# One plain up panel instead of two in each MLP of a two-block transformer kernel, with products summed in one PSUM bank

## What is computed

```python
def rms_norm(x, g):
    xf = x.astype(jnp.float32)
    y = xf * lax.rsqrt(jnp.mean(xf * xf, axis=-1, keepdims=True) + EPS)
    return (y * g.astype(jnp.float32)).astype(x.dtype)

def sq_relu_mlp(h, w_up, w_down):
    return jnp.square(jax.nn.relu(h @ w_up)) @ w_down

    for layer in range(DEPTH):
        ...
        h = h + sq_relu_mlp(rms_norm(h, g_mlp[layer]), w_mlp_up[layer], w_mlp_down[layer])
```

## Time and profile before

| | |
|---|---|
| median of three runs | 1628.29 us (1628.01 to 1630.63) |
| the profiled execution | 1630.15 us, of which the span from first to last instruction is 1628.4 us |
| TensorE busy | 1598.7 us, 98% of the span |
| VectorE, ScalarE, GpSimd busy | 1016.4, 725.8, 271.0 us |
| mean granted TensorE clock | 0.998 |
| TensorE's lines in the MLP | L1650 (products), L1674 (plain panels), L1703 (down panels) |

### The profile page before, as it was taken

The page is one execution under the profiler, slowest core; times in us unless marked ns, Lnnn a source line. Parts: engine busy times, 40 slices in busy tenths (PEclk is TensorE's granted clock), DMA queues, the critical chain, the costliest instruction groups (busy, mean ns, idle before and its releaser), DMA issues.

```text
span 1628.4 us, 29172 instructions
## 1 busy us (share of the span) xinstructions
PE 1598.7 (98%) x12203; PEld 1417.2 (87%) x12203; DVE 1016.4 (62%) x1416; ACT 725.8 (45%) x1144; POOL 271.0 (17%) x222
## 2 busy tenths in 40 slices
PE   8999999999999999999999999999999999989998
PEld 7998677899999999999887898888887788667896
DVE  6534666388666666555557867677756547856544
ACT  5533554465444444331235544444445445675323
POOL 1002212132222222110004222222212000000200
PEclk9999999999999999999999999999999999999999
DMA  6231030123332222232232333222256676001001
GB/s 197 78 78 31 22 84 10 54 78 130 104 104 89 94 84 99 84 99 93 88 104 78 130 104 104 96 90 100 97 103 99 118 96 89 19 1 62 28 28 52
DMA packets 122689, 134.29 MB, mean 82 GB/s; under 512 B 18877, under 2 KB 99508, under 8 KB 122564
## 3 DMA queue, kind: packets, MB, share of 16 engines
q1 hardware_dynamic: 122362, 132.44, 29.7%
...
## 4 chain that ended last, share of the span: by engine, by line
PE 91%; DVE 4%; ACT 2%; issue 1%; DMA 1%; SPq 1%; ACTq 0%; DVEq 0%
PE ps L483 30%; PE ps L1703 22%; PE ps L1650 17%; PE ps L2699 2%; PE ps L829 2%; PE ps L1674 2%; PE ps L812 2%; PE ps L939 1%; PE ps L1220 1%; PE ps L2427 1%; PE ps L837 1%; PE ps L3224 1%; PE ps L2871 1%; PE ps L2850 1%; PE ps L2866 1%
## 5 line engine op out<-in xcount | busy, mean ns | idle before, releaser
L453 ACT ACTIVATE w_hi<-raw 128x1024 fp32r<-128x1024 f32 (+2 forms) x171 | 179.4, 1051 | 400.4 <-PE ps L483 249.4
L483 PE MATMUL ps<-x_hi,w_hi 128*128 128x512 f32 (+4 forms) x872 | 245.8, 333 | 0.5 <-DVE x_lo L503 0.4
L483 PE MATMUL ps<-x_lo,w_hi 128*128 128x512 f32 (+4 forms) x872 | 239.7, 326 | 0.0
L483 PE MATMUL ps<-x_hi,w_lo 128*128 128x512 f32 (+4 forms) x872 | 239.1, 325 | 0.0
L460 DVE TENSOR_TENSOR w_lo<-raw,w_hi 128x1024 fp32r<-128x1024 f32 (+2 forms) x171 | 206.5, 1222 | 45.1 <-ACT w_hi L453 45.1
L1703 PE MATMUL ps<-a_hi,w_hi 128*128 128x258 f32 (+1 forms) x768 | 204.2, 320 | 0.3 <-DVE h L1887 0.3
L1703 PE MATMUL ps<-a_hi,w_lo 128*128 128x258 f32 (+1 forms) x768 | 204.1, 320 | 0.0
L1703 PE MATMUL ps<-a_lo,w_hi 128*128 128x258 f32 (+1 forms) x768 | 204.0, 320 | 0.0
L483 PEld LDWEIGHTS ps<-x_hi,w_hi 128*128 128x128 f32 (+2 forms) x872 | 145.4, 187 | 19.2 <-issue 3.1
L483 PEld LDWEIGHTS ps<-x_lo,w_hi 128*128 128x128 f32 (+2 forms) x872 | 144.6, 186 | 16.4 <-issue 2.2
L483 PEld LDWEIGHTS ps<-x_hi,w_lo 128*128 128x128 f32 (+2 forms) x872 | 144.6, 187 | 14.7
...
## 6 DMA issues: line engine op xcount, KB each, us to landing
raw<-in_w_mlp_up SPq DMA_DIRECT2D x32, 1024.0 KB, 5.3
raw<-in_w_mlp_down SPq DMA_DIRECT2D x32, 1024.0 KB, 5.0
raw<-in_w_in SPq DMA_DIRECT2D x16, 1024.0 KB, 9.6
raw<-in_w_in_conv SPq DMA_DIRECT2D x12, 1024.0 KB, 5.0
raw<-in_w_in_attn SPq DMA_DIRECT2D x8, 1024.0 KB, 5.2
raw<-in_w_out_attn SPq DMA_DIRECT2D x4, 1024.0 KB, 5.0
raw<-in_w_out_conv SPq DMA_DIRECT2D x4, 1024.0 KB, 4.9
raw<-in_w_out SPq DMA_DIRECT2D x4, 1024.0 KB, 5.8
```

The lines of the kernel that those rows point to most:

```text
L453: act.activation(split_tile(w_hi, t), raw_tile(t), ACT.Copy).then_inc(w_hi_ok, 1)
L483: ins = pe.matmul(tile_banks(t)[0:m, b, 0:c], w[:, k, :], x[:, k, x0:x0 + c], start=(k == order[0] and n == 0), stop=(k == order[-1] and n ...
```

## The change

`PLAIN` goes from 2 to 1: up panel 1 of each layer is made of products too. All four groups of mixtures are started during the out projection (the hi part and remainder of the last one follow it), and the weight parts of panel 1 are made under panel 0. The order of the products is 1, 7, 6, 2, 5, 4, 3 now, on three banks: 6, 5 and 3 all add onto bank 0, ScalarE copies product 1 from bank 0 into bank 1 (in PSUM) before 6 starts, and 2 adds onto that copy. VectorE is left with two additions, and evicts two quarters straight from PSUM with relu and scale.

```diff
-        s1, s7, s6, s75 = [at(n, t_off + 1056 * i, [P, HW]) for i, n in enumerate(("s1", "s7", "s6", "s75"))]
+        s7, s6 = [at(n, t_off + 1056 * i, [P, HW]) for i, n in enumerate(("s7", "s6"))]
...
-        ORDER = (1, 5, 7, 2, 6, 3, 4)
+        ORDER = (1, 7, 6, 2, 5, 4, 3)
...
-        P_BANK = {1: 0, 6: 0, 2: 1, 7: 2, 4: 2, 5: 3, 3: 3}
+        P_BANK = {1: 0, 6: 0, 5: 0, 3: 0, 2: 1, 7: 2, 4: 2}
...
-        PLAIN = 2
+        PLAIN = 1
...
         def out_proj_act(act, t0, nxt):
...
-                if j in (4, 6):
-                    mix_hi(act, nxt, j // 2 - 2)
-                if j in (3, 5):
-                    mix_made(act, nxt, j // 2 - 1)
+                if j in (2, 4, 6):
+                    mix_hi(act, nxt, j // 2 - 1)
+                if j % 2:
+                    mix_made(act, nxt, j // 2)
...
         def product_pe(pe, nm, layer, u, m):
...
             if m == 1:
                 pe.wait_ge(w_lo_ok, t + 1)
-                if first:
-                    pe.wait_ge(evicted, MLP_T0[layer] + 2)
-                else:
-                    pe.wait_ge(copied, 3 * n)
-            if m == 5:
+                pe.wait_ge(evicted, MLP_T0[layer] + 1 if first else up_tile(layer, u - 1) + 2)
+            if m == 7:
...
+            if m == 5:
+                pe.wait_ge(copied, 3 * n + 3)
...
+            if m == 3:
+                pe.wait_ge(added, 2 * n + 1)
...
-                    ins = pe.matmul(bank, a[:, w, :], b, start=(k == 0 and j == 0 and m in (1, 2, 7, 5)),
-                                    stop=(k == 3 and j == 2), skip_group_check=m in (6, 4, 3))
+                    ins = pe.matmul(bank, a[:, w, :], b, start=(k == 0 and j == 0 and m in (1, 7)),
+                                    stop=(k == 3 and j == 2), skip_group_check=m not in (1, 7))
...
         def copy_act(act, nm, layer, u, which):
...
-            m, dst = ((1, s1), (7, s7), (6, s6))[which]
+            m, dst = ((1, ps[:, P_BANK[2], :]), (7, s7), (6, s6))[which]
...
         def up_act(act, nm, layer, u):
-            t = up_tile(layer, u)
             if u == 0:
-                mix_made(act, nm, 2)
-                mix_hi(act, nm, 2)
-                split_hi(act, t + 2)
+                mix_hi(act, nm, 3)
+                prep_act(act, layer, 1, 0)
+                prep_act(act, layer, 1, 2)
                 norm_scale(act, nm)
                 square_act(act, nm, layer, 0, 0)
-                mix_made(act, nm, 3)
-                split_hi(act, t + 3)
-                mix_hi(act, nm, 3)
+                prep_act(act, layer, 1, 3)
+                prep_act(act, layer, 1, 1)
                 square_act(act, nm, layer, 0, 1)
             elif u == 1:
+                copy_act(act, nm, layer, 1, 0)
+                copy_act(act, nm, layer, 1, 1)
+                copy_act(act, nm, layer, 1, 2)
                 prep_act(act, layer, 2, 0)
                 prep_act(act, layer, 2, 2)
+                square_act(act, nm, layer, 1, 1)
+                prep_act(act, layer, 2, 3)
                 square_act(act, nm, layer, 1, 0)
-                prep_act(act, layer, 2, 3)
                 prep_act(act, layer, 2, 1)
-                square_act(act, nm, layer, 1, 1)
...
         def add_products(dve, nm, layer, u, what):
...
+                dve.scalar_tensor_tensor(tmp[:, 0, hw:2 * hw], b1, 0.0, scale_bc[:, f + hw:f + 2 * hw], ALU.max, ALU.mult).then_inc(evicted, 1)
...
+                dve.tensor_tensor(tmp[:, 1, 0:hw], s7[:, 0:hw], b0, ALU.add).then_inc(added, 1)
...
+                dve.tensor_tensor(tmp[:, 1, hw:2 * hw], s6[:, 0:hw], b2, ALU.add).then_inc(added, 1)
...
+                dve.scalar_tensor_tensor(tmp[:, 0, 0:hw], b0, 0.0, scale_bc[:, f:f + hw], ALU.max, ALU.mult).then_inc(evicted, 1)
...
         def up_dve(dve, nm, layer, u):
...
             if u == 0:
-                t = up_tile(layer, 0)
-                mix_dve(dve, nm, 2)
-                mix_lo(dve, nm, 2)
+                mix_lo(dve, nm, 3)
+                prep_dve(dve, layer, 1, 0)
+                prep_dve(dve, layer, 1, 2)
                 dve.wait_ge(scale_ok, nm.n + 1)
                 plain_take(dve, nm, layer, 0, 0)
-                split_lo(dve, t + 2)
+                prep_dve(dve, layer, 1, 3)
                 a_low(dve, nm, layer, 0, 0)
-                mix_dve(dve, nm, 3)
+                prep_dve(dve, layer, 1, 1)
                 plain_take(dve, nm, layer, 0, 1)
-                split_lo(dve, t + 3)
-                mix_lo(dve, nm, 3)
                 a_low(dve, nm, layer, 0, 1)
             elif u == 1:
+                add("11")
                 prep_dve(dve, layer, 2, 0)
-                plain_take(dve, nm, layer, 1, 0)
+                add("22")
                 prep_dve(dve, layer, 2, 2)
-                a_low(dve, nm, layer, 1, 0)
-                prep_dve(dve, layer, 2, 3)
-                plain_take(dve, nm, layer, 1, 1)
-                prep_dve(dve, layer, 2, 1)
-                a_low(dve, nm, layer, 1, 1)
+                add("21")
+                scale_dve(dve, nm, layer, 1)
+                add("12")
+                a_low(dve, nm, layer, 1, 1)
+                prep_dve(dve, layer, 2, 3)
+                a_low(dve, nm, layer, 1, 0)
+                prep_dve(dve, layer, 2, 1)
```

93 lines of the change are left out of this document (38 added, 55 removed).

## The result

The changed kernel takes 1659.62 us (median of four runs, 1652.92 to 1660.18), against 1629.03 us for the kernel before beside it: 1.0176 times as long, interval 1.0153 to 1.0200 (the quotient of the two medians is 1.0188). Run again on another occasion it took 1657.43 us (1655.41 to 1659.94) against 1630.00, again a ratio of 1.0176 (1.0159 to 1.0192). The forecast was 1651.6 with a range of 1637 to 1660: the median lies 0.4 us inside the range's upper end, and one of its four runs outside. The profiled execution took 1652.92 us (span 1651.1), the quickest of the four.

The account below looks back on a forecast made before the run. The prediction took the MLP to be bound by TensorE's matmuls. Stalls of 23.6 us, less 3.7 of matmuls, plus 3.4 for the clock, gave +23.3 on 1628.3: 1651.6 us, range 1637 to 1660.

Parts of the forecast that it names:

- Removed matmuls: Second up panel of each layer: 84 half-width matmuls replace the plain ones, gaining 1.73 + 2.00 = 3.7 us.
- Later panels free: Up panels after the first ones: the new product order and the copy into PSUM cost TensorE zero.
- Stall A: Panel 1: TensorE waits before products 1 and 6 for late side work, 7.5 us in layer 0, 7.9 in layer 1.
- VectorE and GpSimd hold each other up: Last activation mix before panel 1: VectorE's operations alternate with GpSimd's sums, making 4.4 us of the layer's first stall.
- Stall C: Product 1 of panel 2 waits for VectorE's last eviction of panel 1: 1.05 us in layer 0, 1.15 in layer 1.
- Stall D: Product 6 of panel 2 waits for its copy, late in ScalarE's queue: 3.0 us in each layer.
- The sum without the clock: Both layers' first panels: 23.6 us of stalls less 3.7 of matmuls, +19.9 us.
- The clock: TensorE's granted clock falls once a layer after idle gaps, costing 3.4 us in all.
- No holding up: Rival: VectorE and GpSimd do not delay each other in the first panels; 1639.4 us, or 1642.8 with clock falls; chance 0.18.
- Full clock: Rival: the stalls come in the first panels but TensorE's clock never falls, 1648.2 us; chance 0.18.
- Faster: Rival: copies reach TensorE in time in the first panels, only the 3.7 us of matmuls show, 1624.6 us; chance 0.05.
- Falls behind both stalls: Rival: the clock falls after the waits in panel 1 and at product 6 of panel 2, each layer, 1655.0 us; chance 0.15.

Follow-up runs that it names:

- reordered kernels: Three versions of the changed kernel: copies and evictions moved earlier and the shared bank alternating, then two VectorE swaps, then earlier GpSimd sums: 1631.19, 1631.70, 1631.27 us.
- filled kernel: Changed kernel with 74 matmuls a layer that nobody reads, put ahead of TensorE's four waits in each layer: 1649.42 us, 1.0123 of the kernel before.
- small sums: Changed kernel with GpSimd's two weight-block sums for panel 1 cut to 8 columns of one block each: 1652.04 us, 1.0133 of the kernel before.

## Why the prediction was right or wrong

**Removed matmuls, 3.7 us: right as a term** of a sum that came out, but never seen by itself: the reordered kernels got 0.8 to 1.3 us of it in their stretches (both layers together), as a short wait or two a layer stayed in each.

**Later panels free: right.** Full windows at 835 matmuls in 100 us, and the loop behind the stretch is the same within 0.2 us. The copy into PSUM takes 0.37, where the bound was 0.39 to 1.0.

**Stall A, 7.5 and 7.9: right, 0.4 too high.** Product 1 came 14.41 us behind the first matmul of panel 0, and 12.40 without a wait (360.02 - 347.62 before): 2.0, put at 2.2. Product 6 came 7.94 behind product 1, and is due after 2.88: 5.1, put at 5.3. Together 7.1; in layer 1 7.5 (14.42 against 12.01, 7.92 against 2.84). Both waits have the named releasers.

**VectorE and GpSimd hold each other up, 4.4 us of A: right in kind, mis-sized.** Each mix step took 1.38 to 1.43 (put at 1.55), and taking panel 1's sums away gave 2.9 us a layer. The rest of the 4.4 was the hold-up by panel 2's sums (1.1), which that experiment leaves in. The Trainium skill's page "SBUF — State Buffer" (SBUF: two separate sides) says that a VectorE operation with two SBUF inputs and a GpSimd operation that reads SBUF exclude each other for a whole instruction. The trace agrees: each mix step ends about one sum later, while the eviction that reads PSUM keeps its 0.68 beside a sum (at 365.80, the sum at 365.50).

**Stall C, 1.05 and 1.15: right, 0.3 to 0.5 too low.** In the filled kernel product 1 of panel 2 starts 8.59 us behind product 6 (8.79 in layer 1), against 7.20 (7.1): 1.4 and 1.7 us. **Stall D, 3.0: right, by two errors that cancel.** Product 6 came 5.72 us behind product 1 of panel 2, due after 2.88: 2.8. But the sum leaves out the copy's own 0.39: 7.85 and its terms make 13.99, so the copy would end at 14.4 and not at 14.05. In the filled kernel product 6 of panel 2 starts 14.32 and 14.51 us behind product 6 of panel 1. D comes out all the same because product 1 of panel 2, from which it is counted, also came 0.3 us later than put (stall C). What the prediction did not say is that C is not paid for itself: with C taken away, D grew by as much or more (1.3 and 1.4 us for waits of 0.92 and 1.18). Sums of stalls along one chain hold only as long as all of them are there.

**The sum without the clock, +19.9: right, closer than its terms.** A is 0.4 too high, C 0.3 to 0.5 too low, and they cancel: that it agrees within 0.2 us is in part luck. The sum gives stretches of 34.27 - 1.73 + 7.5 + 1.05 + 3.0 = 44.09 and 33.91 - 2.00 + 7.9 + 1.15 + 3.0 = 43.96 us. At a full clock, with the idle time filled, they were 44.06 and 44.12, and that kernel took 1649.42, where the rival with a full clock gave 1648.2.

**The clock, 3.4 us: the step that failed.** In the first profile it took (46.19 - 44.06) + (47.07 - 44.12) = 5.1 us in the two stretches: 2.1 in layer 0, 2.95 in layer 1. The price of a fall, 1.7, was near; the number and the places were not. That of layer 0 loses 5 x 0.36 + 5 x 0.32 = 3.4 us of full-speed time, but TensorE is idle for part of it. Of the three in layer 1 the first cost nothing, since product 6 waits for the copy in any case (7.92 us behind product 1, in the filled kernel 7.96); the other two cost 1.5 each. In the two MLPs the whole change thus cost 25.3 us, where the forecast had 23.3.

The median moved by 30.6 (1659.62 - 1629.03), so, with stretches as in the profile, some 5 us of it lie outside the MLPs; and the forecast asked about the clock nowhere else. The three executions at 1659.33 to 1660.18 have a mean granted clock of 0.989 to 0.990 and not 0.993, some 0.0035 x 1655 = 6 us of full-speed time. Falls of the size stand in other profiles, 1.8 us ahead of the first MLP in the second profile of this kernel and about 5 us in the late stage of the reordered one. These three were not profiled, so the place is inferred; and the mean clock is no sure measure, as one execution of the reordered kernel has 0.947 at 1632.15 us. Filling the idle time gives 8 to 10 us back in the median, two to three times what I took; the 3 to 5 us of it beyond the 5.1 lie in places that were not filled, and why they came back is open.

The rule of the Trainium skill that the prediction weighed (page "TensorE: Matmul & The Clock Gate", Why this matters for your kernels: long idle gaps halve the clock) agrees with both profiles of the changed kernel as far as the long wait of stall A goes: the clock is low in or right behind it in all four places. It does not tell the rest: the clock also fell behind product 1's shorter wait, 2.29 us in layer 1 of the first profile and 1.86 in layer 0 of the second, and behind D, some 2.6 us in each layer, it fell in layer 1 alone.

**The rivals.** No holding up: refuted by the small sums. Full clock: refuted by the clock rows, and met when the idle time was filled. Faster: refuted; even with the waits all but removed no gain was measurable. Falls behind both stalls, 1655.0, was nearest to the median, which lies 5 us above it; the profiles show such falls in layer 1 alone.
